# Starting a chunked scan two slots later, with its first four pairs of loads in another order

## The reference

```python
l_mat = jnp.einsum('nbhid,nbhjd->nbhij', kb, kc) * decay_strict
sol = lax.linalg.triangular_solve(eye + l_mat, rhs, left_side=True, lower=True, unit_diagonal=True)
u, w = sol[..., :dv], sol[..., dv:]
attn_intra = jnp.einsum('nbhid,nbhjd->nbhij', qc, kc) * decay_incl
def step(s, xs):
    u_n, w_n, a_n, qd_n, kd_n, gl_n = xs
    v_new = u_n - jnp.einsum('bhcd,bhde->bhce', w_n, s)
    o_n = jnp.einsum('bhcd,bhde->bhce', qd_n, s) + jnp.einsum('bhij,bhje->bhie', a_n, v_new)
    s = s * gl_n[..., None, None] + jnp.einsum('bhcd,bhce->bhde', kd_n, v_new)
    return s, o_n
```

## Time and profile before

| | us |
|---|---|
| median of 3 executions | 1825.86 |
| lowest and highest of them | 1821.56, 1828.45 |
| the profiled execution, its own time | 1828.87 |
| its span in the trace | 1826.5 |
| mean granted TensorE clock | 0.992 |

### The profile page before, as it was taken

One profiled execution on the slowest core, in us unless ns is written; L12 is line 12 of the kernel. 1 busy time (PEld: TensorE's weight loads), 2 busy tenths in 40 slices (PEclk: granted clock), 3 DMA queues, 4 the chain that ended last, 5 costly groups with the idle time before them and its releaser, 6 DMA issues.

```text
span 1826.5 us, 25606 instructions
## 1 busy us (share of the span) xinstructions
PE 1765.2 (97%) x10286; PEld 1448.5 (79%) x10286; DVE 946.2 (52%) x1662; ACT 662.1 (36%) x1212; POOL 277.8 (15%) x421
## 2 busy tenths in 40 slices
PE   5899999999999999899999999999998999999999
PEld 2568888888788888777888887878877788788887
DVE  2435434365324575555556553764457866553334
ACT  5323321133234546344443435422246344232121
POOL 1000000000004466377000003111101010210000
PEclk8999999999999999999999999999999999999999
DMA  9982222223225666744444437667532332752332
GB/s 363 331 288 68 58 56 61 58 81 86 70 58 181 202 180 182 220 130 134 130 125 141 126 91 220 205 210 217 180 115 90 95 100 92 273 193 93 124 118 104
DMA packets 198685, 267.13 MB, mean 146 GB/s; under 512 B 37072, under 2 KB 135625, under 8 KB 197161
## 3 DMA queue, kind: packets, MB, share of 16 engines
q1 hardware_dynamic: 174944, 192.63, 35.0%
q0 software_dynamic: 15552, 58.62, 9.5%
q10 hardware_dynamic: 8073, 14.27, 2.1%
HBM read 221.96 MB, written 43.52 MB: 145 GB/s over the span
## 4 chain that ended last, share of the span: by engine, by line
PE 83%; DVE 7%; ACT 4%; DMA 3%; issue 2%; POOL 1%; SPq 0%; ACTq 0%; DVEq 0%; POOLq 0%
PE psum L1681 24%; PE psum L1682 23%; PE psum L1683 23%; DMA w_raw_mod<-w_mod_dram 2%; PE psum L1792 1%; PE psum L1841 1%; PE psum L1790 1%; DVE w_lo L1108 1%; PE psum L1674 1%; PE psum L1796 1%; PE psum L1794 1%; PE psum L1798 1%; PE psum L2043 1%; ACT square_out L895 1%; ACT w_hi L766 1%
## 5 line engine op out<-in xcount | busy, mean ns | idle before, releaser
L1108 DVE TENSOR_TENSOR w_lo<-w_raw,w_hi 128x1024 fp32r<-128x1024 f32 x232 | 290.4, 1252 | 531.3 <-ACT w_hi L766 531.0
L766 ACT ACTIVATE w_hi<-w_raw 128x1024 fp32r<-128x1024 f32 x232 | 245.7, 1059 | 818.1 <-PE psum L1683 765.3
L1681 PE MATMUL psum<-h_hi,w_hi 128*128 128x512 f32 x1152 | 470.5, 408 | 11.3 <-DVE hc_lo L1162 6.0
L1682 PE MATMUL psum<-h_lo,w_hi 128*128 128x512 f32 x1152 | 453.1, 393 | 0.0
L1683 PE MATMUL psum<-h_hi,w_lo 128*128 128x512 f32 x1152 | 452.5, 393 | 0.0
L1681 PEld LDWEIGHTS psum<-h_hi,w_hi 128*128 128x128 f32 x1152 | 218.3, 189 | 70.6 <-issue 24.8
L1683 PEld LDWEIGHTS psum<-h_hi,w_lo 128*128 128x128 f32 x1152 | 217.6, 189 | 47.9
L1682 PEld LDWEIGHTS psum<-h_lo,w_hi 128*128 128x128 f32 x1152 | 218.6, 190 | 36.4
L1177 DVE SCALAR_TENSOR_TENSOR conv_acc<-conv_in,convw,conv_acc 128x772 f32<-128x772 f32 x96 | 98.2, 1023 | 3.4
L1681 PE MATMUL psum<-w_hi,m_hi 128*128 128x512 f32 x256 | 99.6, 389 | 0.0
L1682 PE MATMUL psum<-w_lo,m_hi 128*128 128x512 f32 x256 | 99.6, 389 | 0.0
(11 more groups left out here) (323 smaller groups left out, 2821.7 us busy)
## 6 DMA issues: line engine op xcount, KB each, us to landing
w_raw<-w_in_dram SPq DMA_DIRECT2D x168, 512.0 KB, 3.9
w_raw_mod<-w_mod_dram SPq DMA_DIRECT2D x64, 512.0 KB, 6.1
w_raw_modg<-w_mod_dram POOLq DMA_DIRECT2D x32, 512.0 KB, 4.6
w_raw<-w_out_dram SPq DMA_DIRECT2D x32, 512.0 KB, 3.7
gate_scratch<-gate_stage ACTq DMA_DIRECT2D x48, 256.0 KB, 4.3
w_raw<-w_proj_a_dram SPq DMA_DIRECT2D x16, 512.0 KB, 4.0
w_raw<-w_proj_b_dram SPq DMA_DIRECT2D x16, 512.0 KB, 3.8
gates<-gate_scratch POOLq DMA_DIRECT2D x32, 256.0 KB, 4.2
```

What stands on the lines that cost most here:

```text
L766: act.activation(part(whi[i % 2], p), part(place, p), ACT.Copy).then_inc(S("w_hi"), 1)
L1108: dve.tensor_tensor(part(wlo[i % 2], p), part(raw_of(n)[0], p), part(whi[i % 2], p).bitcast(f32), ALU.subtract).then_inc(S("w_lo"), 1)
L1681: pe.matmul(out_ap, lh, rh, start=first, stop=False, skip_group_check=shared)
L1682: pe.matmul(out_ap, lh, rl, start=False, stop=False, skip_group_check=shared)
```

## The change

Three things. The pairs of the scan begin at kk 128, two slots later than before (126); the slots stay in their order. The loads of L and of the k rows for pair 0 move one piece ahead on SP, right behind the last spill of scores. The two loads of inverted blocks stay behind the next piece's load, and the wait until the spilled scores have landed comes behind them.

```diff
@@ scan_plan
             end += 11 if lat else 8
-    end += 6
+    end += 8
@@ scan_transfers
-                if kk == PAIRS[0]["at"] - 6:
-                    sp.wait_ge(S("block_in"), 16 * N_UNITS)
+                if kk == PAIRS[0]["at"] - 9:
                     sp.wait_ge(S("diagonal"), N_UNITS)
                     sp.wait_ge(S("l_out"), 16 * N_UNITS)
                     load_L(0)
                     sp.wait_ge(S("k_rows_out"), 16 * N_UNITS)
                     load_k_rows(0)
+                if kk == PAIRS[0]["at"] - 7:
+                    sp.wait_ge(S("block_in"), 16 * N_UNITS)
+                    load_unit(0)
                     sp.wait_ge(S("scores_out"), 16 * N_LAT)
-                    load_unit(0)
```

## The result

The changed kernel takes 1830.7 us (median of 6 executions, 1829.1 to 1833.5), the kernel before 1824.6 in the same measurement: ratio 1.0031, interval 1.0019 to 1.0042. By the ratio it is slower by 5.7 us (3.5 to 7.7). The forecast was 1822.9, with a range to 1830.0. The change stays within 0.5%, but it goes the other way, and the time lies above the range.

A forecast was written before the change was run, and what follows sets the result against it. PE is busy 97% of the span, so only its stalls and low clock could give time back. Scan start -4.4, pairs' phase -1.2 and behind the scan +2.6 make -3.0 us: from 1825.86 to 1822.9, range 1817.0 to 1830.0.

The forecast's parts named there:

- Term 1, wait: Start of the scan: PE's wait before the first couple5 falls from 5.83 to 2.0 us, so -3.8.
- with the same 7.1 us: Start of the scan: the second load of inverted blocks takes 7.1 us as before and lands at 774.1.
- which gives 772.7: Start of the scan: weight piece issued at 765.5 takes the k rows' 7.2 us, landing just in time for ACT at 772.75.
- Rival 1: Start of the scan: piece or inverted blocks land 1.1 us later than taken; PE waits 3.1 us; time 1824.6; chance 0.18.
- The split as the floor of 2.0 us: Start of the scan: DVE's split precedes the transposes, so couple5 cannot start before 776.0 and PE waits 2.0 us.
- Term 1, clock: Start of the scan: the low clock after the stall cost 2.3 us and would cost 1.7, so -0.6.
- Term 2: Pairs' new phase against the pieces: correct5's wait in context pair 3 goes, -1.2 us; all eight latent pairs 0.
- Rival 4: Latent pairs: their new phase stalls PE, each losing 1.2 us: +9.3, net +6.3, time 1832.2; chance 0.08.
- Term 3, wait: Behind the scan: POOL's row starts 2.7 us later, b_mod holds DVE's split longer, PE waits 2.0 us more.
- some of SP's weight load gets through ahead of it: Behind the scan: SP's 512 KB load, 1.4 us, partly precedes POOL's row, so its end moves 2.0 us instead of 2.7.
- Term 3, clock: Behind the scan: clock loss after the longer stall rises from 1.7 us to at most 3.1; taken as +0.6.
- Rival 3: Behind the scan: the stall grows by the full 2.7 us and clock loss to 3.1: +4.1, time 1824.4; chance 0.08.

## Why the prediction was wrong, point by point

**What bounds the kernel** was right: PE's waits at the start of the scan and behind it, and the clock after them. Over the table, the time follows the column "lost" (9.8 to 20.9 us against 1820.6 to 1830.7), with single profiles up to 2.5 us off a straight line.

**Term 1, wait (-3.8).** This is the largest miss. Measured, as means of two profiles each: 5.7 to 4.6, so -1.1. The step that failed here is "with the same 7.1 us" for the blocks and "which gives 772.7" for the piece. Both took the landing times of neighbours that stood elsewhere in SP's row. In the changed kernel's two profiles the piece took 9.4 and 8.1 us, and ACT waited 5.95 and 4.72 us for it. It was also issued 0.9 us later than forecast: 770.43, less the 4.01 us by which this execution runs behind (ACT's `w_hi` at 771.32 instead of 767.31), is 766.4 and not 765.5, as the two issues of L took SP 1.86 us instead of 0.81. Rival 1 had the mechanism, a late landing that holds couple5 (with a wait of 3.1), and the wait was longer still. The piece's old time from issue to landing was 5.3 us, and the 1 MB now ahead of it is 3 us at 350 GB/s, so an estimate of 8.3 was at hand. The rule of the Trainium skill that spoke against the change ("DMA: Bandwidth & Descriptors", "Queues, rings and completion order") is that a DMA engine takes the descriptors of one ring in order; the traces agree with it, with 9.4 and 8.1 us. The mistake was to add the 3 us to the old landing, though the issue moved later as well, and so to call the two readings equal. The split as the floor of 2.0 us was right: 2.21 and 1.96 in the two kernels in which no load was late.

**Term 1, clock (-0.6).** Measured 2.3 and 2.5 before, 2.1 and 2.5 after: 0.

**Term 2 (-1.2 and eight zeros).** The eight latent pairs are 0 as predicted: from 900 to 1100 us PE is idle 3.5 and 3.6 us before, 3.5 and 3.6 after. Rival 4 did not come. The -1.2 was mostly chance: the repeated kernel before has 0.4 at that place, and the changed one none and, at pair 1, which has that phase now, 0.4. As means of two that is 0.8 to 0.2, so -0.7.

**Term 3, wait (+2.0, bounds 1.3 to 2.7).** The second step that failed. The wait grew from 2.3 to 5.3 us as means of two, +3.0, outside the bounds. That POOL's row starts 2.7 us later and that b_mod holds DVE was right. Wrong was the discount, "some of SP's weight load gets through ahead of it". SP issues a weight piece at 1109.5 us in the trace of before, 5.3 us behind the row's first load (1104.22), and in the changed kernel at 1111.6, still 2.5 us behind it (1109.06). So in neither kernel did this piece get ahead of the row. It lands sooner (after 10.4 and 10.6 us instead of 13.1 and 13.2), but the next piece of SP lands later (10.9 and 11.0 instead of 9.1 and 9.3). The row keeps its length: from its first load to DVE's first sum it takes 18.3 and 19.1 us before, 19.1 and 18.9 after. So its end moved by the whole 2.7 of its start, and the remaining 0.3 is within what two executions differ by. With 2.7 the term would have been right within its spread.

By the Trainium skill ("DMA: Bandwidth & Descriptors", "Queues, rings and completion order") a DMA engine takes turns between the rings that it has work for, and by that rule the forecast had named the full 2.7. With 3.0 the traces agree with it better than with 2.0.

**Term 3, clock (+0.6).** Measured 1.6 and 0 before, 2.4 and 2.7 after: +1.8. The 1.7 from which the forecast started was one execution's.

**The sum.** -1.1 + 0 - 0.7 + 3.0 + 1.8 = +3.0 us where -3.0 was forecast; the column "lost" has +3.3 as means of two (17.4 to 20.7), and the time +4.6 (2.7 to 6.4) in the longer measurement. That is within the interval; where the rest lies, if it is more than noise, is not shown. Neither term turned the sign by itself: with term 1 as measured the forecast would have been +0.3, with term 3 as measured -0.8. Rival 3 was the right one in kind, the tail eats the gain, but it was priced with the forecast's own bounds and with term 1 whole. No rival had both terms wrong at once, though both hang on the same thing, what a transfer in a full stretch costs, and so fail together. Two sums of the prediction are also off, without bearing on this: eight pairs at 1.2 us are 9.6 and not 9.3, and with all its bounds the forecast's own range is about 1819.9 to 1825.8 instead of 1820.5 to 1825.5.

## What to carry to other kernels

When slots are moved against a steady stream of pieces, list every row of loads that is released by the last slot as well as those ahead of the first: here the gain at the head was 1 us and the cost at the far end 5. A landing time read from a full stretch belongs to a place in a queue, not to a tile; when the order changes, add up the bytes ahead in the same row, from the new time of issue. A small load that an engine needs (8 KB of b_mod) was better placed ahead of the bulk in its row: that edit took 6.2 us off the changed kernel. Before the next edit, read again which piece waits and for what: the last run moved loads out of b_mod's way when the wait that was left belonged to a weight piece of another row.

## What the runs showed of the hardware

What a short stall costs in clock can't be read from its length here. Behind the scan the table's fourteen profiles have five waits of 1.8 to 2.8 us that cost 1.6, 0, 0, 1.2 and 1.4 us in clock, two of 3.6 and 4.8 us that cost 1.4 and 1.3, and three of 5.2 to 5.5 us that cost 2.4 to 3.0; waits of 1.0 and 1.6 us cost nothing. Before the first couple5 one wait of 2.21 us cost nothing and one of 1.96 us 1.7. The window around the first of these has the granted clock at 1.00 (third number from the end), against 0.52 in the earlier trace rows:

```profile
776.00:782.00 6.00, 4.18 (x57) 3.81 (x58) 3.52 (x12) 3.69 (x12) 5.22 (x11) 1.00 0.70 237
```

A 512 KB load landed after 3.7 to 3.9 us in a quiet stretch (1099 to 1104 us in the profiles of the two kernels) and, in the same profiles, after 9 to 13 us beside POOL's row. Loads of 2 KB behind 2.5 MB in their own row needed 7.1 to 8.7 us (medians of four); with the kv rows behind them 4.7 in the kernel before and 5.7 in the changed one.
